# Key norm in an RWKV block: the row sums as small products inside the receptance piece, the inverse root on GpSimd, spread by products

## The reference

```python
r, k, v = jnp.einsum('nbtc,ncd->nbtd', jnp.stack([xr, xk, xv]), w_rkv)
w = -jax.nn.softplus(-(w0 + jnp.tanh(xw @ w1) @ w2)) - 0.5
a = jax.nn.sigmoid(a0 + (xa @ a1) @ a2)
kk = heads(k * k_k)
kk = kk / jnp.maximum(jnp.sqrt(jnp.sum(kk * kk, -1, keepdims=True)), 1e-12)
k = k * (1 + (a - 1) * k_a)
```

## Time and profile before

| | us |
|---|---|
| median of 3 executions | 1507.2 |
| lowest and highest | 1506.49 and 1508.62 |
| the profiled execution, its own time | 1507.1 |
| its span in the trace | 1505.2 |
| PE busy in the span | 1403.7 |
| DVE busy | 883.4 |
| ACT busy | 630.7 |
| POOL busy | 78.5 |

### The profile page before, as it was taken

The page is one execution under the profiler, slowest core; times in us unless marked ns, Lnnn a source line. Parts: engine busy times, 40 slices in busy tenths (PEclk is TensorE's granted clock), DMA queues, the critical chain, the costliest instruction groups (busy, mean ns, idle before and its releaser), DMA issues.

```text
span 1505.2 us, 21641 instructions
## 1 busy us (share of the span) xinstructions
PE 1403.7 (93%) x9280; PEld 1256.9 (84%) x9280; DVE 883.4 (59%) x1292; ACT 630.7 (42%) x899; POOL 78.5 (5%) x43
## 2 busy tenths in 40 slices
PE   7989899997899999999999999899988888699998
PEld 4676898996899997876789999898988887599997
DVE  5168435426744547555564545798998756465555
ACT  1343342434443345444444344533434544544443
POOL 0011030001200002100110000100000000000000
PEclk9999999998999999999999999998999999999999
DMA  9422000005565553623175555644543434255550
GB/s 287 145 74 112 1 1 1 1 1 196 168 196 181 183 189 116 227 88 109 35 244 191 175 195 168 192 132 141 167 140 126 155 112 156 68 183 181 185 193 28
DMA packets 154383, 204.96 MB, mean 136 GB/s; under 512 B 7440, under 2 KB 128400, under 8 KB 154160
## 3 DMA queue, kind: packets, MB, share of 16 engines
q1 hardware_dynamic: 154288, 203.59, 41.3%
HBM read 202.53 MB, written 1.05 MB: 135 GB/s over the span
## 4 chain that ended last, share of the span: by engine, by line
PE 72%; DVE 20%; ACT 5%; issue 1%; DMA 0%; SPq 0%; DVEq 0%; ACTq 0%
PE PS L464 17%; PE PS L465 17%; PE PS L466 17%; DVE PH L1999 6%; DVE WL L1561 4%; PE PS L765 3%; PE PS L752 3%; PE PS L769 2%; PE PS L668 2%; DVE AL L1588 2%; PE PS L613 1%; PE PS L718 1%; DVE PA L1812 1%; ACT WH L1098 1%; PE PS L633 1%
## 5 line engine op out<-in xcount | busy, mean ns | idle before, releaser
L1561 DVE TENSOR_TENSOR WL<-RG,WH 128x2048 fp32r<-128x2048 f32 x163 | 372.4, 2291 | 218.4 <-ACT WH L1098 218.4
L464 PE MATMUL PS<-AH,WH 128*128 128x256 f32 x1664 | 481.1, 289 | 17.6 <-DVE AL L1588 13.8
L465 PE MATMUL PS<-AL,WH 128*128 128x256 f32 x1664 | 476.2, 286 | 0.0
L466 PE MATMUL PS<-AH,WL 128*128 128x256 f32 x1664 | 475.7, 286 | 0.0
L1098 ACT ACTIVATE WH<-RG 128x2048 fp32r<-128x2048 f32 x164 | 311.3, 1906 | 95.8 <-PE PS L466 95.7
L464 PEld LDWEIGHTS PS<-AH,WH 128*128 128x128 f32 x1664 | 324.5, 195 | 24.6 <-issue 12.8
L465 PEld LDWEIGHTS PS<-AL,WH 128*128 128x128 f32 x1664 | 324.9, 195 | 1.7 <-issue 0.2
L466 PEld LDWEIGHTS PS<-AH,WL 128*128 128x128 f32 x1664 | 324.7, 195 | 0.0
L464 PE MATMUL PS<-WH,HH 128*128 128x512 f32 x304 | 118.8, 391 | 0.1
L465 PE MATMUL PS<-WL,HH 128*128 128x512 f32 x304 | 118.7, 390 | 0.0
L466 PE MATMUL PS<-WH,HL 128*128 128x512 f32 x304 | 118.3, 389 | 0.0
(11 more groups left out here) (269 smaller groups left out, 1779.7 us busy)
## 6 DMA issues: line engine op xcount, KB each, us to landing
RG<-in_ffn_w_in SPq DMA_DIRECT2D x44, 1024.0 KB, 5.2
RG<-in_w_ff SPq DMA_DIRECT2D x32, 1024.0 KB, 5.4
RG<-in_w_in SPq DMA_DIRECT2D x30, 1024.0 KB, 5.2
RG<-in_ffn_w_down SPq DMA_DIRECT2D x22, 1024.0 KB, 4.9
RG<-in_w_rkv SPq DMA_DIRECT2D x12, 1024.0 KB, 5.5
RG<-in_moba_w_qkv SPq DMA_DIRECT2D x12, 1024.0 KB, 5.3
RG<-in_w_o SPq DMA_DIRECT2D x4, 1024.0 KB, 9.0
RG<-in_wx_kv SPq DMA_DIRECT2D x4, 1024.0 KB, 5.8
```

The lines of the kernel that those rows point to most:

```text
L464: e.matmul(o, lh, rh, start=start, stop=False)
L465: e.matmul(o, lh, rl, start=False, stop=False)
L466: return e.matmul(o, ll, rh, start=False, stop=stop)
L1561: v.tensor_tensor(WL[:, lo_n % NW, :], ring(SPLIT[lo_n]), WH[:, lo_n % NW, :].bitcast(F32), ALU.subtract).then_inc(s_lo, 1)
```

## The change

The norm takes another way. The squares `qq` become the weights of four products with `sel2`, a constant of two columns, one column per head of the block. The result has tokens in partitions and 8 columns: (2 blocks of channels) x (2 blocks of tokens) x (2 heads). These four products stand between the two halves `m` of the receptance piece. VectorE bounds the 128x8 sums from below by 1e-24 and GpSimd raises them to the power -0.5. VectorE copies the 8 columns into 128x512, each repeated 64 times. Four products of this tile with the identity turn it back into channels by tokens, in PSUM, and VectorE multiplies `kk` by it. ScalarE's square root and VectorE's bound and reciprocal over 128x512 go away.

```diff
@@ tensor_program
+            def norm_sums(j):
+                e.wait_ge(s_kq, j + 1)
+                if j:
+                    e.wait_ge(s_ks, j)
+                for q in range(4):
+                    t = e.matmul(PS[6][:, 2 * q:2 * q + 2], qq[:, q * 128:q * 128 + 128], cst('sel2'), start=True, stop=True)
+                t.then_inc(s_nm, 1)
...
                     for m in range(2):
+                        if (n, m) == (1, 1):
+                            norm_sums(j)
                         for k in range(8):
...
-                e.wait_ge(s_kq, j + 1)
-                if j:
-                    e.wait_ge(s_nr, j)
-                e.matmul(PS[6][:, :], cst('bones'), qq, start=True, stop=True).then_inc(s_nm, 1)
+                e.wait_ge(s_nq, j + 1)
+                for q in range(4):
+                    t = e.matmul(PS[6][:, q * 128:q * 128 + 128], qq[:, q * 128:q * 128 + 128], ident, start=True, stop=True)
+                t.then_inc(s_nb, 1)
                 if j:
                     bonus(j - 1)
...
                     if tt:
-                        e.wait_ge(*((s_nr, 4), (s_rs_, 4))[h])
+                        e.wait_ge(*((s_ks, 4), (s_rs_, 4))[h])
@@ scalar_program
-                s.wait_ge(s_nm, j + 1)
-                s.activation(qq, PS[6][:, :], ACT.Sqrt, bias=0.0, scale=1.0).then_inc(s_nr, 1)
@@ vector_program
+                v.wait_ge(s_nm, j + 1)
+                v.tensor_scalar(RN, PS[6][:, 0:8], 1e-24, None, ALU.max).then_inc(s_nx, 1)
+                v.wait_ge(s_nr, j + 1)
+                v.tensor_copy(v3(qq, 64), RN.unsqueeze(2).broadcast_to([128, 8, 64])).then_inc(s_nq, 1)
                 if j:
                     bonus(j - 1)
-                v.wait_ge(s_nr, j + 1)
-                own_dve(v.tensor_scalar(qq, qq, 1e-12, None, ALU.max))
-                own_dve.done()
-                own_dve(v.reciprocal(qq, qq))
-                own_dve.done()
-                own_dve(v.tensor_tensor(kk, kk, qq, ALU.mult))
+                v.wait_ge(s_nb, j + 1)
+                own_dve(v.tensor_tensor(kk, kk, PS[6][:, :], ALU.mult))
@@ gpsimd_program
+            own_pool(g.memset(ST[:, 184:192], -0.5))
...
+                g.wait_ge(s_nx, j + 1)
+                own_pool.done()
+                g.tensor_tensor(RN, RN, ST[:, 184:192], ALU.pow).then_inc(s_nr, 1)
```

More of the change, by code:

```diff
@@ L173, in build @@
         s_kr, s_dz, s_dt, s_mid, s_ee = (sem(n) for n in ("kr_mm", "decay_mm", "decay_tanh", "decay_mid", "decay_exp"))
-        s_kq, s_nm, s_nr, s_rs_, s_gr, s_gk = (sem(n) for n in ("k_sq", "k_norm_mm", "k_norm", "r_out", "r_decayed", "k_decayed"))
+        s_kq, s_nm, s_nx, s_nr, s_nq, s_nb, s_rs_, s_gr, s_gk = (sem(n) for n in ("k_sq", "k_norm_mm", "k_sumsq", "k_rnorm", "k_rnorm_wide", "k_rnorm_mm", "r_out", "r_decayed", "k_decayed"))
         s_ks, s_yp, s_bm, s_bv = (sem(n) for n in ("k_scaled", "rk_out", "bonus_mm", "bonus_out"))
@@ L257, in build @@
         w2v, a2v = P2[0:64, 0:1024], P2[0:64, 1024:2048]
+        RN = ST[:, 192:200]
         mid, nmid, em = ST[:, 32:36], ST[:, 36:40], ST[:, 40:44]
```

## The result

| | before | after | forecast |
|---|---|---|---|
| median of 6 executions each, us | 1504.74 | 1536.36 | 1527 |
| lowest and highest | 1500.69 and 1508.62 | 1533.93 and 1539.62 | range 1518 to 1535 |
| ratio | | 1.0202, interval 1.0182 to 1.0222 | |
| the profiled execution, its own time | 1507.1 | 1533.93 | 1526.9 |
| its span | 1505.2 | 1532.1 | |

The ratio is taken over all executions; the two medians divide to 1.0210, inside the interval.

A forecast was written before the change was run, and what follows sets the result against it. The prediction took the rounds' chain through ScalarE and VectorE as the bound, TensorE having slack there. `bonus(3)` 21.2 us late less 1.4 given back made 19.8, added to 1507.1: 1526.9, say 1527; range 1518 to 1535.

The forecast's parts named there:

- No table loads in rounds 1 to 3: ScalarE at round starts: removing Sqrt ends the function switches, saving 1.3 us in each of rounds 1 to 3.
- The tanh wait: ScalarE waits for the decay products about 6.4 us behind each square from round 1 on.
- norm leg: Between decay and wide products: bound 0.2, power 0.7, wide copy 0.6 and hand-overs, 1.75 us per round.
- Given back behind `bonus(3)`: After the gate: TensorE at full clock, bonus and transposes save about 1.1, the first inversion a little; 1.4 us.
- rival 4: GpSimd's first power alone pays for code fetching, priced at 4.86 us once; 1531 us, chance 0.03.
- The 6 us: First GpSimd call of a freshly loaded kernel pays about 6 us without a profile instruction; by that, 1533 us.
- Rivals 1 and 2: 1: tanh not delayed, 8 us faster, 1499, chance 0.03. 2: a later wait absorbs the shift, about 1507, chance 0.03.
- rival 3: GpSimd's power computed element by element, 4.2 us more in each of four rounds; 1544 us, chance 0.06.
- The power: GpSimd's 128x8 power in each round: 0.7 us, the middle between ends of 0.10 and 1.36.
- short idle: TensorE's wait before round 3's wide and bonus products, which were then priced at 1.3 us each.
- The high end of the range: Power 1.36, copy 0.69, new products at half clock, nothing given back, round 0 copy beside GpSimd's product: 1534.6 us.
- the sums' place: Sums between receptance halves delay the tanh: sums 1.0, half piece 3.5, decay products 1.95, together 6.45 us.

The follow-up runs named there:

- e6: Changed kernel plus ten extra GpSimd operations at its start, power and product over 128x1, 8, 32, 128 and 512; 1587.78 us.
- e10: Changed kernel with idle TensorE products before the wide-copy wait and the gate's third quarter in round 3's key-piece bank; 1526.22 us, ratio 1.0152.
- e11: Changed kernel with GpSimd's power made a constant product, idle TensorE products before the wide-copy wait, gate's third quarter in round 3's key-piece bank; 1518.27 us.
- e2: Changed kernel with GpSimd's power replaced by a product with a constant, so the norm is not computed; 1528.18 us, ratio 1.0146.
- e1: Changed kernel with the four sums moved back behind the receptance piece and decay products (round 3: behind the forms); 1531.29 us, ratio 1.0163.
- e5: Kernel before, with only its product with `bones` moved between the halves of the receptance piece; 1534.95 us, ratio 1.0187.
- e4: Changed kernel with sums behind the decay products, wide products and bonus behind the next round's whole key piece; 1517.6 us, ratio 1.0081.
- e7: Changed kernel with queues rearranged: sums behind decay products, wide products inside the next key piece, bonus, receptance product and gate reordered; 1507.17 us, ratio 1.0012.
- e9: Changed kernel with GpSimd's power made a constant product and 6, 5, 5, 2 idle TensorE products before the wide-copy wait; 1528.11 us, ratio 1.0142.
- e8: Kernel before, with a dummy ScalarE exponential behind the receptance copy to load the table early; 1503.15 us, ratio 0.9973.

## Why the forecast was right in sign and too small

**Right.** No table loads in rounds 1 to 3. The tanh wait (7.53, 6.62) for the decay products, which stand behind sums, half piece and square. TensorE waits 7.36, 6.39 and 6.38 for the wide copy (5.7 said). The norm leg stands behind the decay, the bonus behind the wide products, the gate's second half behind `k_scaled`. The sums take 0.95 to 1.05. Given back behind `bonus(3)` are 1.7 (1.4 said), and the inversions pass the shift on: the first product behind the first transposes starts at 193.96 and not 166.96, and the span ends 26.9 later. The first power costs no more than the next (1.65, 1.64), so rival 4 falls. The 6 us that the forecast cites from the Trainium skill do not show as a gap either: the first power starts 0.07 us behind the bound, as the others do. Rivals 1 and 2 fall by the sign; rival 3 has the right cause (the cost grows with the number of elements, e6) and a size too large.

**The terms that were too small.** The milestones show where the excess arises:

| | forecast | measured | excess |
|---|---|---|---|
| round 1 starts | 87.35 | 88.76 | 1.4 |
| round 2 | 114.85 | 118.13 | 3.3 |
| round 3 | 141.7 | 146.60 | 4.9 |
| last step of round 3 ends | 172.3 | 179.74 | 7.4 |
| `bonus(3)` | 174.5 | 181.98 | 7.5 |

- The power: 1.65, not 0.7, four times: 3.8, half of it all. It lies above the high end of 1.36 too. The bound took a product of 128x512 as the most; e6 shows that the power goes by a different law than a product, 0.157 us per column, so a product of any size was no bound. Its size in the time is shown by e10 and e11, whose stages differ by 5.74 for 4 x 1.45 = 5.8 of the rows. The medians differ by more, 8.0 there and 8.2 between the change and e2; what that more is, the traces do not settle.
- GpSimd beside VectorE: L1826 takes 1.14 and not 0.69 in rounds 1 to 3 (1.35 together), missed; the copy of round 0 takes 1.39 (0.8 over its 0.6), named only in the bounds. The other three copies take 0.43, which gives 0.5 back. Net 1.6.
- The clock: wide products 2.07 each time (1.9 said, 1.3 in round 3), bonus products 1.72 in the chain (1.5, 1.3 in round 3). That is 3 x 0.17 + 0.77 + 2 x 0.22 + 0.42 = 2.1. Behind the gap the clock is 0.50 through all eight products (106.90 to 111.00), in round 3 too, where the forecast took the wait (a "short idle", 3.51 us) as nearly harmless.

3.8 + 1.6 + 2.1 is 7.5, against 7.4 at the last step. Some tenths more in the key piece behind the gaps, and 0.4 less ahead of round 0's decay, nearly cancel. So the step that failed is the price of the power, 0.7 us a time in the forecast and 1.65 in the trace, with the clock behind the gap second. With the three terms as measured and 1.7 given back, the sum comes to 1534.1, against the 1533.93 of the profiled execution.

The high end of the range had the power at 1.36, all new products at half clock and GpSimd beside VectorE in round 0, and came to 1534.6, which is above the profiled execution. The power at 1.65 would have added 4 x 0.29 = 1.2. What it left out besides is the spread: it was worked out for one execution, and the six lie from 1533.93 to 1539.62.

**The reason behind the sign was only half right.** The forecast put the loss down to the sums' place, by which the tanh come late. e1 takes the place back and gains 5, not the 19 that this would ask. What costs is a closed loop: with the new norm TensorE waits for VectorE's copy with nothing between, then VectorE for TensorE; with the place alone TensorE waits for the square. Either part of the change closes it (e1, e5). In the changed kernel it opens when the next key piece is put into the wait (the stage is 13.3 us shorter in e4 and 25.0 in e7).

## What to carry to other kernels

When work moves from one engine to another inside a loop, write down the loop of waits once around and ask what each engine does meanwhile: here each of two parts alone cost over 20 us and both together only 27, so undoing one shows little. Price an operation without a row by its law and not by the size of its tile, and where a bound is worked out from another kind of operation, say that it is no bound. A stall that is shortened on one engine may come up as a short gap elsewhere; look at the granted clock behind each gap that remains before calling a gain missing.

## What the hardware showed unexpectedly

- GpSimd's power costs 0.156 to 0.161 us per column of 128 partitions on a base of 0.4: 1.65 for 8 columns, 82.14 for 512. A product of 8 columns takes 0.20, one of 32 takes 0.25.
- A GpSimd product makes VectorE's operation beside it longer: the copy takes 1.39 for 0.43 and the three-operand step 1.14 for 0.69 beside one of 1.18 us; in e7 four scans take 2.31 for 1.37 beside one of 1.37. The Trainium skill ("SBUF — State Buffer", SBUF: two separate sides) has one pair of ports that a GpSimd operation, or a VectorE one in a two-port mode or with two inputs in SBUF, holds for its whole length. The rows agree: GpSimd's product runs from 78.91 to 80.09, and the copy, which starts at 78.97 and takes 0.43 when alone, ends at 80.36, after it; L1826 ends at 113.33, after the product that ends at 112.78. VectorE's product with `kk` (L1823, 111.47), which reads PSUM, keeps its 0.68 beside the same product.
- The same gap of 1.42 us ahead of the same products was followed by clock 0.59 (118 to 122 us) in one execution (e9) and by 1.00 in another (e11).
- The stretch from the first product of the inversions to the end took 1338.2 us in the trace of before and 1333.0 in that of e10. From 100 to 200 us behind that product the mean granted clock was 0.93 in the first and 0.95 in the second.
- ACT_TABLE_LOAD takes 1.28 in every row of e8 and of before, and a dummy operation moves it off the chain (e8).
